# A hybrid decoder trunk on one core: attention with token-major values and 64-row score products, column sums in one wide product, pooling in quadrants

## The chip, the core and the metric

The kernel runs on one core of a Trainium2 chip. The metric is the device time of one execution in microseconds. The kernel before took 896.11 us as the median of three runs (891.52, 896.11, 896.16).

The engines are named as the profile names them: PE is TensorE (PEld its weight loads), DVE VectorE, ACT ScalarE, POOL GpSimd, SP the queue that issues most transfers.

## The reference, cut to what matters

All data is f32. One layer over 1024 tokens of width 1024: a normalised and modulated input `h` is projected by `w_in`; the columns of the projection feed four mixers (pooling, sliding-window attention, gated convolution, RWKV time mixing); their outputs are joined, projected by `w_out` and added to x. A mixture of 32 experts follows. The change lies in the projection, the attention, the pooling, and in the modulation vector that the second half of the layer needs.

```python
mod = cond @ w_ada[l] + b_ada[l]          # six vectors of 1024: sh1 sc1 gt1 sh2 sc2 gt2
p = h @ w_in[l]
# attention: 4 query heads, 2 key/value heads of 64, window 128, blocks of 128 tokens
qb = q.reshape(B, nb, 128, KVH, G, hd) * (hd ** -0.5)
s = jnp.einsum('bnqhgd,bnkhd->bnhgqk', qb, kb)     # k over this block and the one before
s = s - slopes[:, :, None, None] * dist            # and masked by the window
p = exp(s - m); p = p / (sum(p) + exp(sink - m))
o = jnp.einsum('bnhgqk,bnkhd->bnqhgd', p, vb)
# pooling: 4 groups of 64 channels, each with a 64x64 matrix
y = jnp.einsum('btgc,gce->btge', d, w_pool)
```

## The kernel before, in words

The program is written engine by engine; every dependence is a semaphore, and the order on each engine is the order of the code.

**Projection.** `project` (L853) makes one block of 128 projected columns for all 1024 tokens: the stationary operand is a 128x128 tile of `w_in` (`win[:, par, k, :]`), the moving one is 512 tokens of `hT` (the input, channels on the partitions), two halves by eight steps of k, 16 products in PS banks 0 and 1 or 2 and 3. ACT moves out the first half of the tokens and DVE the second (`projected`) into `pT`, which is [channel, block, token]. There are 19 blocks in the order of `ORDER`: two of queries, the keys, the values (i = 3), then pooling, convolution and RWKV.

**Attention in slots.** From block i = 5 on, each `project` has a piece of the attention beside it (L931 to L952), and this document calls that stretch a slot. In a slot PE runs, in this order: `outputs(nb)` (probabilities by values), `scores(nb + 2)`, the first half of a `project`, `flip_probs(nb + 1)` (the probabilities turned by 8 transposes), `sums(nb + 2)`, the second half of the `project`. A Fori loop of two turns holds the slots nb = 0 to 3; the slots nb = 4 and 5 are written out behind it, and the slots for nb = 6 and 7 have only `outputs`, `project` and, for the first, `flip_probs`.

- `scores` (L871) takes a query tile `qz` with the 64 rows of the other key head at zero (ACT builds it in `queries`, with the factor 1/8), so each of the 4 heads is one product over all 128 rows with 256 keys. Then it transposes two tiles of values (`vs`, copied by ACT) into PS bank 6, from which ACT (`values`) makes `vt`.
- `outputs` (L900) makes 8 products of 128 rows by 64 columns, in the order head, key block; heads 0 and 2 land in partitions 0 to 63, heads 1 and 3 in 64 to 127.
- `sums` (L914) adds over the partitions what DVE gathered in `acb` (512 columns of the modulation per slot, `half_blocks`, L1810: 16 operations on 256 columns). For the gate vectors (nb = 0, 1, 6, 7) it is one wide product of a tile of ones by `acb`; for the shift and scale vectors (nb = 2 to 5, the slots of the loop) eight products with a single moving column each, whose stationary operand is 64 strided columns of `acb`. DVE adds the bias (`gate_columns` or `mod_columns`).

**DVE's order in a slot** (L1837): `projected`, `attended` (copy of the outputs), `softmax`, `flipped`, `mod_columns`, `half_blocks`. In `softmax` it waits for ACT's exponentials. `flip_probs` on PE waits for `att_nm` of the newest scores, which `softmax` gives once it has read them.

**Pooling and convolution** run on POOL from the moment that block 11 is projected (L620 to L650). `pooled` (L955) then multiplies each half of the pooled channels by a 128x128 matrix that holds two 64x64 blocks on its diagonal, two products of 512 tokens each; `pooled(0)` stands ahead of block 16 and `pooled(1)` behind it.

Of the kernel before, what the change touches and what calls it, by code (L numbers as in the profile page):

```python
# [114 lines left out]
def build(nc, w, out):  # L115
    ctx = ExitStack()
    with ctx:
# [38 lines left out]
        qz, o = area(REG_W, A_ATT, 4, P)  # L156
        vs, o = area(REG_W, o, 2 * P)
        vt, o = area(REG_W, o, 2, 2, P)
        sc, o = area(REG_W, o, 2, 4, 2 * P)
# [189 lines left out]
        def identb(n):  # L349
# [11 lines left out]
                 "att_q att_qk att_vps att_v  att_nm att_p att_pn att_tp att_tpa att_tpd att_o att_y "  # L361
# [418 lines left out]
        def _(pe):  # L780
# [89 lines left out]

            def scores(nb):  # L871
                first = isinstance(nb, int) and nb == 0
                k0 = 1 if first else 0
                ks = slice(nb * P + (PAD - P * (1 - k0)), nb * P + PAD + P) if isinstance(nb, int) else \
                    ds(nb * P + (PAD - P), 2 * P)
# [12 lines left out]

            def flip_probs(nb, par, nxt=True):
                k0 = 1 if isinstance(nb, int) and nb == 0 else 0  # L890
# [9 lines left out]
            def outputs(nb, par):  # L900
                k0 = 1 if isinstance(nb, int) and nb == 0 else 0
# [12 lines left out]
            def sums(nb, gates, half=0):  # L914

                pe.wait_ge(s["acb_ready"], nb * 2 + 2)
                pe.wait_ge(s["att_v"], nb + 1)
# [10 lines left out]
            for i in range(2, SLOT0):  # L928
                project(i % 2, 32 * (i // 2 + 1), i - 1, shifted=i == 2)
# [3 lines left out]
            project(1, 32 * 3, 4, lambda: sums(0, True))  # L933
            scores(1)
            project(0, 32 * 4, 5, lambda: (flip_probs(0, 0), sums(1, True)))

            def beside(g, u, gates):

                outputs(g * 2 + u, u)
                scores(g * 2 + (2 + u))  # L940
                project((1 + u) % 2, g * 32 + 32 * (4 + u), g * 2 + (6 + u),
                        lambda: (flip_probs(g * 2 + (1 + u), (1 + u) % 2), sums(g * 2 + (2 + u), gates, u)))

            with pe.Fori(0, 2) as g:
                for u in range(2):
                    beside(g, u, False)
            for u in range(2):
                beside(2, u, True)
            outputs(6, 0)
            project(1, 32 * 7, 12, lambda: flip_probs(7, 1, False))  # L950
            outputs(7, 1)
# [3 lines left out]
            def pooled(c):  # L955
# [420 lines left out]
        def _(act):  # L1376
# [43 lines left out]
            def projected(i, par, blk=None):  # L1420
# [6 lines left out]
                else:  # L1427
                    fn(dst, PS[2 * par][:, :]).then_inc(s["proj_act"], 1)


            def queries(nb):
                first = isinstance(nb, int) and nb == 0
                k0 = 1 if first else 0
                tok = slice(nb * P + PAD, nb * P + PAD + P) if isinstance(nb, int) else ds(nb * P + PAD, P)
                at = slice(nb * P + PAD - P * (1 - k0), nb * P + PAD + P) if isinstance(nb, int) else ds(nb * P + (PAD - P), 2 * P)
                if not first:
                    act.wait_ge(s["att_qk"], nb)
                    act.wait_ge(s["att_vps"], nb)
                for kv in range(2):
                    r = slice(64 * kv, 64 * kv + 64)  # L1440
                    fn(qz[r, 2 * kv:2 * kv + 2, :], pT[r, B_Q:B_Q + 2, tok], scale=float(HD) ** -0.5)
                fn(vs[:, k0 * P:], pT[:, B_VAL, at]).then_inc(s["att_q"], 1)

            def values(nb, par):
                k0 = 1 if isinstance(nb, int) and nb == 0 else 0
                act.wait_ge(s["att_vps"], nb + 1)
                fn(vt[:, par, k0:, :], PS[6][:, k0 * P:256].rearrange("p (a b) -> p a b", b=P)).then_inc(s["att_v"], 1)
# [15 lines left out]
            for i in range(2, N_ATT):  # L1463
                projected(i, i % 2)
            act.wait_ge(s["proj_dve"], N_ATT)
            act.wait_ge(s["proj_act"], N_ATT)
            for n in range(2):
                queries(n)
                projected(SLOT0 - 1 + n, n)
                values(n, n)  # L1470
# [3 lines left out]
            with act.Fori(0, 3) as g:  # L1474
                for u in range(2):
                    queries(g * 2 + (2 + u))
                    projected(g * 2 + (6 + u), u, g * 2 + (B_BG + u))
                    values(g * 2 + (2 + u), u)
# [4 lines left out]
            def pooled(c):  # L1483
                act.wait_ge(s["pool_ps"], c + 1)
# [167 lines left out]
        def _(dve):  # L1652
# [96 lines left out]
            dve.wait_ge(s["ss_ready"], NT)  # L1749
            dve.wait_ge(s["hT_tr"], NT)  # L1750
# [501 lines left out]
```

## Time and profile before

| | us |
|---|---|
| median of three runs | 896.11 |
| lowest and highest run | 891.52, 896.16 |
| span of the profiled execution | 890.9 |
| PE busy | 837.5 (94%) |
| DVE busy | 453.4 (51%) |
| POOL busy | 277.5 (31%) |
| ACT busy | 252.9 (28%) |

The profile is one execution; its span runs from the first to the last instruction, and its own total isn't given apart from it: it lies 0.6 us below the lowest run and 5.2 us below the median. PE is busy over nearly the whole span, so the reading starts with what PE does, and goes by the starts of its groups: the end of a product in the profile is modelled, the start of the next group isn't. The profile records every f32 product as two matmul records, and every transpose as one.

### The profile page before, as it was taken

What the parts mean: (1) busy time and instruction counts of PE and PEld (TensorE: products, weight loads), DVE (VectorE), ACT (ScalarE), POOL (GpSimd) and SP (SyncE); (2) the same over time, 40 slices, a digit from 0 to 9 for tenths busy, and PEclk for the clock granted to TensorE, in tenths of its full rate; (3) what the DMA queues carried; (4) which work ended last, traced back from release to release, by engine and by line L of the source; (5) the groups of instructions that cost most, each with busy time, mean ns of one, the idle gap of its engine ahead of it and who ended that gap; (6) DMA issues with size and microseconds to landing.
All of it is one profiled execution on the core that took longest, in us unless ns stands there. A gap on an engine that the chain in (4) does not pass through costs nothing.

```text
span 890.9 us, 17159 instructions
## 1 busy us (share of the span) xinstructions
PE 837.5 (94%) x7046; PEld 561.2 (63%) x7046; DVE 453.4 (51%) x1146; ACT 252.9 (28%) x613; POOL 277.5 (31%) x265
## 2 busy tenths in 40 slices
PE   5999999999999999899999999999999999999950
PEld 5754445555544444788788555555788888888830
DVE  3830467777741133667674243443664555555534
ACT  5310122222210140564543122223222322323214
POOL 4810000000099800615524000000035556544232
PEclk9899999999999999999999999999999999999985
DMA  9923543334300120300000492111889999988639
GB/s 343 282 80 102 162 136 120 118 118 142 118 24 25 47 71 0 146 3 4 4 3 5 179 403 104 47 48 56 314 296 306 295 287 272 283 263 266 211 70 368
DMA packets 79638, 136.32 MB, mean 153 GB/s; under 512 B 17134, under 2 KB 51147, under 8 KB 79563
## 3 DMA queue, kind: packets, MB, share of 16 engines
q1 hardware_dynamic: 69258, 118.44, 38.3%
q0 software_dynamic: 10304, 16.82, 7.9%
q8 instruction: 55, 0.90, 0.4%
q14 instruction: 21, 0.16, 0.1%
HBM read 124.18 MB, written 29.92 MB: 173 GB/s over the span
## 4 chain that ended last, share of the span: by engine, by line
PE 90%; DMA 3%; DVE 3%; issue 2%; ACT 1%; SPq 0%; DVEq 0%; POOLq 0%; POOL 0%; ACTq 0%
PE bank L782 84%; PE bank L1330 3%; DMA REG_Y<-in_x 2%; DVE REG_P L2227 1%; DMA REG_P<-y_d 1%; PE bank L896 1%; PE bank L1261 1%; DMA REG_Y<-xn_d,tbl 1%; DMA y_d<-REG_Y,idx 1%; PE bank L1029 0%; DVE REG_P L1969 0%; DVE REG_P L1951 0%; ACT REG_W L1378 0%; ACT REG_Y L1378 0%; PE bank L886 0%
## 5 line engine op out<-in xcount | busy, mean ns | idle before, releaser
L782 PE MATMUL bank<-REG_W 128*128 128x512 f32 (+1 forms) x736 | 273.4, 542 | 0.0
L782 PEld LDWEIGHTS bank<-REG_W 128*128 128x128 f32 (+1 forms) x736 | 118.0, 181 | 138.1 <-issue 137.6
L782 PE MATMUL bank<-REG_W,REG_Y 128*128 128x512 f32 x256 | 118.3, 599 | 1.4 <-DVE REG_Y L2182 1.1
L1378 ACT ACTIVATE REG_P<-bank 128x256 f32<-128x256 f32 (+2 forms) x126 | 53.4, 462 | 154.8 <-PE bank L782 132.1
L1378 ACT ACTIVATE REG_Y<-bank,mod,s 128x128 f32<-128x128 f32 x136 | 51.1, 456 | 86.8 <-PE bank L1330 86.8
L782 PE MATMUL bank<-REG_P 64*64 64x64 f32 (+1 forms) x2816 | 69.3, 223 | 6.5 <-issue 4.5
L782 PEld LDWEIGHTS bank<-REG_W,REG_Y 128*128 128x128 f32 x256 | 45.6, 191 | 44.3 <-issue 44.2
L782 PEld LDWEIGHTS bank<-REG_Y,REG_W 128*128 128x128 f32 (+1 forms) x640 | 65.7, 181 | 7.1 <-issue 7.1
L782 PEld LDWEIGHTS bank<-REG_P 64*64 64x64 f32 x2816 | 60.9, 134 | 14.4 <-issue 6.7
L782 PE MATMUL bank<-REG_Y,REG_W 128*128 128x128 f32 (+1 forms) x640 | 69.0, 276 | 0.2 <-DVE REG_Y L2051 0.2
L626 POOL TENSOR_TENSOR REG_P<-REG_P 128x1040 f32<-128x1040 f32 x2 | 4.8, 2390 | 187.1 <-DVE REG_P L1765 187.0
L782 PE MATMUL bank<-REG_Y,REG_P 128*128 128x128 f32 x496 | 58.2, 275 | 0.0
L782 PEld LDWEIGHTS bank<-REG_Y,REG_P 128*128 128x128 f32 x496 | 56.7, 192 | 0.7 <-issue 0.7
L1674 DVE SCALAR_TENSOR_TENSOR REG_Y<-REG_P,cc,REG_Y 128x256 f32<-128x256 f32 x112 | 54.3, 485 | 4.0
L719 POOL DMA_INDIRECT y_d<-REG_Y,tbl x22 | 34.9, 1588 | 59.9 <-DVE REG_Y L2190 59.9
L782 PE MATMUL bank<-REG_P,REG_Y 128*128 128x512 f32 x112 | 51.4, 592 | 0.0
L668 POOL TENSOR_TENSOR REG_P<-REG_P,lmask 128x512 f32<-128x512 f32 x20 | 25.8, 1300 | 78.7 <-DVE REG_P L1960 78.4
L2051 DVE TENSOR_SCALAR REG_Y<-bank,s,mod 128x128 f32<-128x128 f32 x136 | 46.2, 404 | 2.7 <-PE bank L1330 2.7
L571 POOL TENSOR_SCALAR ss<-ss 128x1 f32<-128x1 f32 x16 | 3.8, 238 | 137.2 <-ACT REG_P L1378 127.8
L2179 DVE SCALAR_TENSOR_TENSOR REG_Y<-REG_Y,bank 128x128 f32<-128x128 f32 x33 | 9.5, 288 | 70.5 <-issue 45.5
L1378 ACT ACTIVATE REG_Y<-bank 128x128 f32<-128x128 f32 (+2 forms) x43 | 14.9, 347 | 101.7 <-PE bank L782 61.7
L2190 DVE SCALAR_TENSOR_TENSOR REG_Y<-bank,tbl,gtb 128x512 f32<-128x512 f32 x46 | 32.4, 747 | 19.3 <-PE bank L782 16.8
(296 smaller groups left out, 1168.1 us busy)
## 6 DMA issues: line engine op xcount, KB each, us to landing
REG_P<-in_w_ada SPq DMA_DIRECT2D x18, 1024.0 KB, 6.3
REG_W<-in_w_in SPq DMA_DIRECT2D x17, 512.0 KB
REG_P<-in_moe_w_gate SPq DMA_DIRECT2D x17, 512.0 KB
REG_W<-in_moe_w_gate SPq DMA_DIRECT2D x16, 512.0 KB
REG_W<-in_moe_w_up SPq DMA_DIRECT2D x16, 512.0 KB
REG_W<-in_moe_w_down SPq DMA_DIRECT2D x16, 512.0 KB
REG_P<-in_moe_w_up SPq DMA_DIRECT2D x14, 512.0 KB
REG_P<-in_w_ada SPq DMA_DIRECT2D x3, 2048.0 KB, 12.4
```

What stands on the lines that cost most here:

```text
L668: gp.tensor_tensor(bl[:, l % 2], ab[:, :, 0, :], lmask[:, l:l + 1, :].to_broadcast([P, 8, CH]), ALU.mult)\
L719: gp.indirect_dma_start(out=y_d[:, :], out_offset=bass.IndirectOffsetOnAxis(ap=at, axis=0), in_=yo[b], in_offset=None, bounds_check=last_r ...
L782: return pe.matmul(o_, l, r, start=start, stop=stop, skip_group_check=True)
L896: last = pe.transpose(PS[4 + h // 2][:, ((h % 2) * 2 + kb) * P:((h % 2) * 2 + kb + 1) * P], sc[:, par, h, kb * P:(kb + 1) * P], ident[:, :])
L1261: last = pe.transpose(PS[4 + k // 4][:, (k % 4) * P:(k % 4 + 1) * P], strided[:, k, :], ident[:, :])
L1330: last = pe.transpose(PS[k // 4][:, (k % 4) * P:(k % 4 + 1) * P], xg[b][:, k * P:(k + 1) * P], ident[:, :])
L1378: return act.activation(o_, i_, f, **kw)
L1674: last = stt(dst, src[:, k], cc[:, k:k + 1], dst, ALU.mult, ALU.add)
L2051: last = ts(dst[:, k, :], PS[bank][:, (k - 4) * P:(k - 3) * P], s2[:, k:k + 1], mod[:, M_SH2 + k:M_SH2 + k + 1], ALU.mult, ALU.add)
L2179: ch.step(stt(a1[:, par, :], th[:, par, :], 1.0, PS[2 + par][:, 0:P], ALU.add, ALU.mult))
L2190: last = stt(yo[b][:, h * 512:(h + 1) * 512], PS[4 + 2 * par + h][:, :], gate(TURN[e] if isinstance(e, int) else e), gtb[:, 1, h * 512:(h ...
L2227: stt(x1[:, j], x1[:, j], rs[:, 2, j:j + 1], fg, ALU.mult, ALU.mult).then_inc(s["f_o"], 1)
```

## The change

Five edits. (1) The values (block 3) are projected with the operands swapped: the stationary tile is 128 tokens of `hT`, the moving one 128 columns of `w_in`, so they come out with tokens on the partitions, 64 products of 128 columns instead of 16 of 512; the two transposes per block, `vs`, `vt` and ACT's copies go. (2) `scores` multiplies only the 64 rows of the head's key head, for key heads 0 and 1 in turn, into banks 4 and 5; `qz` and ACT's `queries` go, the factor 1/8 is put into the copy of the query blocks. (3) `outputs` alternates between the two column halves from product to product, reads the values from `pT`, and leaves out the empty key block for nb = 0. (4) `sums` is the wide product for all eight; `mod_columns` on DVE picks the columns out of the wide result by a product with a mask of one diagonal and a reduction. (5) `pooled` makes four 64x64 products of 512 tokens instead of two full ones. PE's loop is written out, three memsets of DVE go.

```diff
+            def values(loads, done):
+                pe.wait_ge(s_win[1], loads)
+                pe.wait_ge(s["proj_act"], done)
+                pe.wait_ge(s["proj_dve"], done)
+                for j in range(NT):
+                    for k in range(KD):
+                        last = mm(PS[2 + j // 4][:, (j % 4) * P:(j % 4 + 1) * P], hT[:, k, j * P:(j + 1) * P], win[:, 1, k, :],
+                                  k == 0, k == KD - 1)
+                last.then_inc(s["proj_ps"], 1)
             def scores(nb):
...
-                pe.wait_ge(s["att_q"], nb + 1)
-                if not isinstance(nb, int) or nb >= 2:
+                if nb == 0:
+                    pe.wait_ge(s["proj_act"], N_ATT - 1)
+                    pe.wait_ge(s["proj_dve"], N_ATT - 1)
+                if nb == 1:
+                    pe.wait_ge(s["att_nm"], 1)
+                if nb >= 2:
                     pe.wait_ge(s["att_tpa"], nb - 1)
                     pe.wait_ge(s["att_tpd"], nb - 1)
-                for h in range(4):
-                    last = mm(PS[4 + h // 2][:, (h % 2) * 256 + k0 * P:(h % 2) * 256 + 256], qz[:, h, :], pT[:, B_KEY, ks])
-                last.then_inc(s["att_qk"], 1)
-                if not first:
-                    pe.wait_ge(s["mod2_ready"], nb)
-                for kb in range(k0, 2):
-                    last = pe.transpose(PS[6][:, kb * P:(kb + 1) * P], vs[:, kb * P:(kb + 1) * P], ident[:, :])
-                last.then_inc(s["att_vps"], 1)
+                for a in range(2):
+                    for kv in range(2):
+                        r = slice(64 * kv, 64 * kv + 64)
+                        last = mm(PS[4 + kv][:, a * 256 + k0 * P:a * 256 + 256], pT[r, B_Q + a, tok], pT[r, B_KEY, ks])
+                        if a == 1:
+                            last.then_inc(s["att_qk"], 1)
...
-                if isinstance(nb, int) and nb == NT - 1:
+                if nb >= 1:
                     pe.wait_ge(s["att_y"], nb)
-                for h in range(4):
-                    r = 64 * (h % 2)
+                for kv in range(2):
                     for kb in range(k0, 2):
-                        last = mm(PS[7][r:r + 64, (h // 2) * P:(h // 2 + 1) * P], vt[:, par, kb, (h // 2) * HD:(h // 2 + 1) * HD],
-                                  ptT[:, h, kb, :], kb == k0, kb == 1)
-                last.then_inc(s["att_o"], 1)
+                        at = PAD + (nb - 1 + kb) * P + kv * HD
+                        for a in range(2):
+                            last = mm(PS[7][64 * a:64 * a + 64, kv * P:(kv + 1) * P], pT[:, B_VAL, at:at + HD],
+                                      ptT[:, 2 * kv + a, kb, :], kb == k0, kb == 1)
...
+            def sums(nb):
                 pe.wait_ge(s["acb_ready"], nb * 2 + 2)
-                pe.wait_ge(s["att_v"], nb + 1)
-                if gates:
-                    last = mm(PS[6][:, :], ones[:, :], acb.rearrange("p a b -> p (a b)"))
-                else:
-                    strided = acb.rearrange("p a (q k) -> p k (a q)", k=KD)
-                    for k in range(KD):
-                        last = mm(PS[6][64 * half:64 * half + 64, k:k + 1], strided[:, k, :], ones[:, 0:1])
-                last.then_inc(s["mod2_ps"], 1)
+                if nb >= 1:
+                    pe.wait_ge(s["mod2_ready"], nb)
+                mm(PS[6][:, :], ones[:, :], acb.rearrange("p a b -> p (a b)")).then_inc(s["mod2_ps"], 1)
...
-                for h in range(2):
-                    last = mm(PS[6 + h][:, :], pw[:, c, :], pmd[:, c, h * 512:(h + 1) * 512])
-                last.then_inc(s["pool_ps"], 1)
+                for h, g in ((0, 0), (1, 1), (1, 0), (0, 1)):
+                    r = slice(64 * g, 64 * g + 64)
+                    last = mm(PS[6 + h][r, :], pw[r, c, r], pmd[r, c, h * 512:(h + 1) * 512])
+                    if h != g:
+                        last.then_inc(s["pool_ps"], 1)
...
-            dve.memset(ptT[:, :, 0, :], 0.0)
-            dve.memset(vt[:, 0, 0, :], 0.0)
-            dve.memset(qz, 0.0)
...
-                tt(mod[r, ds(g * KD + M_SH2, KD)], PS[6][r, 0:KD], pq[r, ds(g, 1), :].rearrange("p o k -> p (o k)"), ALU.add)\
+                ch.step(tt(pick[r], PS[6][r, :].rearrange("p (q k) -> p q k", k=KD),
+                           identq[r, :].unsqueeze(2).to_broadcast([64, HD, KD]), ALU.mult))
+                ch.step(dve.tensor_reduce(picked_k[r, :], pick[r].rearrange("p q k -> p k q"), AX.X, ALU.add))
+                tt(mod[r, ds(g * KD + M_SH2, KD)], picked_k[r, :], pq[r, ds(g, 1), :].rearrange("p o k -> p (o k)"), ALU.add)\
                     .then_inc(s["mod2_ready"], 1)
```

## Rows read from the trace of the kernel before

**Rows 1.** Page, the span in 40 slices: granted TensorE clock in tenths.
```profile
PEclk9899999999999999999999999999999999999985
```
**Rows 2.** Chain that ended last, 60 to 330 us, by line.
```profile
by line: PE bank L782 97.1%; PE bank L896 2.4%; PE bank L886 0.6%
```
**Rows 3.** Timeline, PE, one loop slot: start us, us, what, xrecords.
```profile
145.10 7.03 PE L782 MATMUL bank<-REG_W 128*128 128x512 f32 x16
151.97 1.04 PE L896 MATMUL bank<-ident,REG_W 128*128 128x128 f32 x8
152.94 2.08 PE L782 MATMUL bank<-ones,REG_Y 128*64 128x1 f32 x16
154.95 7.13 PE L782 MATMUL bank<-REG_W 128*128 128x512 f32 x16
162.01 1.15 PE L782 MATMUL bank<-REG_Y,REG_W 128*64 128x128 f32 x16
163.09 1.99 PE L782 MATMUL bank<-REG_P,REG_W 128*128 x8
164.92 0.38 PE L886 MATMUL bank<-ident,REG_W 128*128 128x128 f32 x2
165.14 0.59 PE L782 MATMUL bank<-REG_W 128*128 128x512 f32 x1
```
**Rows 4.** Timeline, PE, a slot behind the loop, with the wide sum.
```profile
232.98 1.02 PE L782 MATMUL bank<-REG_Y,ones 128*128 128x512 f32 x2
233.84 7.03 PE L782 MATMUL bank<-REG_W 128*128 128x512 f32 x16
240.80 1.14 PE L782 MATMUL bank<-REG_Y,REG_W 128*64 128x128 f32 x16
```
**Rows 5.** Timeline, PE, the scores of block 0.
```profile
109.31 1.05 PE L782 MATMUL bank<-REG_P,REG_W 128*128 128x128 f32 x8
110.21 0.27 PE L886 MATMUL bank<-ident,REG_W 128*128 128x128 f32 x1
110.31 7.03 PE L782 MATMUL bank<-REG_W 128*128 128x512 f32 x16
```
**Rows 6.** Timeline, PE, expert stage: products of 128 columns, each with new weights.
```profile
709.11 3.74 PE L782 MATMUL bank<-REG_Y,REG_P 128*128 128x128 f32 x32
712.68 1.88 PE L782 MATMUL bank<-REG_S,REG_Y 128*128 128x512 f32 x4
```
**Rows 7.** Timeline, PE, RWKV stage: products on 64x64 quadrants.
```profile
358.06 1.10 PE L782 MATMUL bank<-REG_W,REG_P 64*64 64x128 f32 x32 [0.27 <-DVE REG_P L1951]
359.09 1.16 PE L782 MATMUL bank<-cen,REG_P 128*128 128x128 f32 x8
```
**Rows 8.** Timeline, DVE, the same loop slot as rows 3.
```profile
145.09 1.42 DVE L1786 SCALAR_TENSOR_TENSOR REG_W<-adist,bank 128x256 f32<-128x256 f32 x4 [0.42 <-PE bank L782]
...
148.07 0.16 DVE L1792 TENSOR_SCALAR nm<-mx 128x4 f32<-128x4 f32 x1
...
150.88 1.14 DVE L1797 TENSOR_SCALAR REG_W<-REG_W,rd 128x256 f32<-128x256 f32 x4
...
155.37 0.35 DVE L1672 TENSOR_SCALAR REG_Y<-REG_P,cc 128x256 f32<-128x256 f32 x1
...
163.19 0.68 DVE L1765 COPY REG_P<-bank 128x512 f32 x1
163.79 0.41 DVE L1779 COPY REG_Y<-bank 128x256 f32 x1
```
**Rows 9.** Timeline, DVE, slot of block 0: a reduction and a read of bank 6.
```profile
111.32 0.69 DVE L1789 TENSOR_REDUCE mx<-REG_W 128x4 f32<-128x512 f32 x1
...
118.24 0.69 DVE L1821 TENSOR_TENSOR gtb<-gtb,bank 128x512 f32<-128x512 f32 x1 [2.66 <-PE bank L782]
```
**Rows 10.** Timeline, PE: the second pooling product.
```profile
319.46 1.88 PE L782 MATMUL bank<-REG_Y,pw 128*128 128x512 f32 x4
```
**Rows 11.** Timeline, POOL: its last pooling operation.
```profile
307.49 2.35 POOL L650 TENSOR_TENSOR REG_Y<-REG_Y,REG_P 128x1024 f32<-128x1024 f32 x1
```

More of the change, by code:

```diff
@@ L360, in build @@
                  "proj_k proj_ps proj_act proj_dve pad_ready acc_ready acb_ready "
-                 "att_q att_qk att_vps att_v  att_nm att_p att_pn att_tp att_tpa att_tpd att_o att_y "
+                 "att_qk att_nm att_p att_pn att_tp att_tpa att_tpd att_o att_y "
                  "pool_d pool_ps pool_y conv_y  "
@@ L878, in scores @@
+            def scores(nb):
+                k0 = 1 if nb == 0 else 0
+                tok, ks = slice(nb * P + PAD, nb * P + PAD + P), slice(nb * P + PAD - P * (1 - k0), nb * P + PAD + P)
+                if nb == 0:
[4 more added lines that the diff above has]
+                if nb >= 2:
                     pe.wait_ge(s["att_tpa"], nb - 1)
                     pe.wait_ge(s["att_tpd"], nb - 1)
-                for h in range(4):
-                    last = mm(PS[4 + h // 2][:, (h % 2) * 256 + k0 * P:(h % 2) * 256 + 256], qz[:, h, :], pT[:, B_KEY, ks])
@@ L889, in flip_probs @@
             def flip_probs(nb, par, nxt=True):
-                k0 = 1 if isinstance(nb, int) and nb == 0 else 0
+                k0 = 1 if nb == 0 else 0
                 pe.wait_ge(s["att_pn"], nb + 1)
@@ L898, in flip_probs, with outputs @@
                 last.then_inc(s["att_tp"], 1)
-            def outputs(nb, par):
-                k0 = 1 if isinstance(nb, int) and nb == 0 else 0
-                pe.wait_ge(s["att_v"], nb + 1)
+            def outputs(nb):
+                k0 = 1 if nb == 0 else 0
+                if nb == 0:
+                    pe.wait_ge(s["proj_act"], N_ATT)
+                    pe.wait_ge(s["proj_dve"], N_ATT)
                 pe.wait_ge(s["att_tpa"], nb + 1)
                 pe.wait_ge(s["att_tpd"], nb + 1)
-                if isinstance(nb, int) and nb == NT - 1:
+                if nb >= 1:
@@ L906, in outputs @@
                     pe.wait_ge(s["att_y"], nb)
[L907 to L908 removed]
+                for kv in range(2):
                     for kb in range(k0, 2):
[L910 to L924 removed]
+                        at = PAD + (nb - 1 + kb) * P + kv * HD
+                        for a in range(2):
+                            last = mm(PS[7][64 * a:64 * a + 64, kv * P:(kv + 1) * P], pT[:, B_VAL, at:at + HD],
+                                      ptT[:, 2 * kv + a, kb, :], kb == k0, kb == 1)
+                            if kv == 1 and kb == 1:
+                                last.then_inc(s["att_o"], 1)
@@ L926, in _ @@
+            def sums(nb):
+                pe.wait_ge(s["acb_ready"], nb * 2 + 2)
+                if nb >= 1:
+                    pe.wait_ge(s["mod2_ready"], nb)
+                mm(PS[6][:, :], ones[:, :], acb.rearrange("p a b -> p (a b)")).then_inc(s["mod2_ps"], 1)
             first_block()
             second_block()
-            for i in range(2, SLOT0):
-                project(i % 2, 32 * (i // 2 + 1), i - 1, shifted=i == 2)
+            project(0, 32 * 2, 1, shifted=True)
+            values(32 * 2, 2)
@@ L931, in _ @@
+            project(0, 32 * 3, 3)
             pe.wait_ge(s["sel_ready"], 1)
             scores(0)
-            project(1, 32 * 3, 4, lambda: sums(0, True))
+            project(1, 32 * 3, 4, lambda: sums(0))
             scores(1)
[L935 to L949, printed above, removed]
+            project(0, 32 * 4, 5, lambda: (flip_probs(0, 0), sums(1)))
+            for nb in range(NT - 2):
+                outputs(nb)
+                scores(nb + 2)
+                project((nb + 1) % 2, 32 * (nb // 2) + 32 * (4 + nb % 2), nb + 6,
+                        lambda: (flip_probs(nb + 1, (nb + 1) % 2), sums(nb + 2)))
@@ L950, in _ @@
+            outputs(6)
             project(1, 32 * 7, 12, lambda: flip_probs(7, 1, False))
-            outputs(7, 1)
+            outputs(7)
             project(0, 32 * 8, 13)
@@ L1427, in projected @@
                 else:
[L1428 to L1447, printed above, removed]
+                    fn(dst, PS[2 * par][:, :], scale=scale).then_inc(s["proj_act"], 1)
             def exps(nb, par):
@@ L1462, in _ @@
             first_projected(1)
[L1463 to L1466, printed above, removed]
+            projected(2, 0, scale=float(HD) ** -0.5)
+            projected(3, 1)
             for n in range(2):
-                queries(n)
                 projected(SLOT0 - 1 + n, n)
-                values(n, n)
                 exps(n, n)
@@ L1763, in projected @@
                     pT[:, ds(blk, 1), PAD + 512:PAD + 1024].rearrange("p o t -> p (o t)")
+                if blk is None and i == N_ATT - 2:
+                    ts(dst, PS[2 * par + 1][:, :], float(HD) ** -0.5, None, ALU.mult).then_inc(s["proj_dve"], 1)
+                    return
                 if blk is not None or i not in MIXED:
```

25 lines of the change are left out of this document (8 added, 17 removed).

## The prediction, written before the changed kernel was timed

> **What bounds the kernel now.** I read the page's slices first: PE is busy in tenths of nine over almost the whole span at a granted clock of nine tenths or more in nearly every slice, the upper of its two levels, 2.4 GHz [rows 1]. Then the chain of work that ended last, for the stretch the change touches: from 60 to 330 us it consists of PE alone, row after row [rows 2], and no PE wait stands in the view of waits there. So any time taken from PE's own stream in this stretch shortens the stretch one for one, until another engine comes late. Last the timeline of PE, where the starts of the groups give prices. A loop slot lasts from 145.10 to 165.14, 20.04 us [rows 3].
>
> **Unit prices.** Half a projection is 8 products of 512 columns, 16 records: 151.97 - 145.10 = 6.87 us, 0.429 a record, 0.859 a product [rows 3]. The time goes with the moving columns: 256 columns are 0.429 a product, 128 are 0.215. A series of 128-column products with new weights for each takes (712.68 - 709.11)/32 = 0.1116 us a record [rows 6], so nearly all of the weight load is hidden. A change of the array's shape also has a price: the same half projection lasts 6.87 between full products, 6.96 if the 64-column outputs follow [rows 4], and 7.06 if 64-column products stand on both sides [rows 3]. That is 0.10 for each change of shape.
> The Trainium skill (TensorEngine Tiling (Array Packing), Key Properties) says that a change of tiling mode drains the engine. The trace agrees, and 0.10 us is the size of it here.
>
> **1. Values token-major.** 64 products of 128 columns, 128 records by 0.1116 = 14.28 us [rows 6], in place of 16 by 0.859 = 13.74 [rows 3]: +0.54. All on the path. It can't be under 13.74, the columns being the same; if no load were hidden, the eight single-column products would be the nearest price, 2.01/16 = 0.126 a record [rows 3], 16.1, or +2.4. The expert rows are the same form, so I take +0.54.
> The transposes of values go: 0.10 for block 0 [rows 5], and 0.22 (164.92 to 165.14) [rows 3] for seven more: -1.64. ACT's copies go too, at nothing: PE never waits for them now.
>
> **2. Scores of 64 rows.** Now four products of 256 columns, 1.73 without the change of shape, 1.83 behind the outputs (163.09 to 164.92) [rows 3]. With rows 0 to 63 and 64 to 127 at work together there are two rounds of 0.429, 0.86, plus 0.10 on each side: 1.06. Six blocks behind outputs save 0.77 each, 4.62; block 1 saves 1.73 - 1.06 = 0.67; block 0 goes from 0.90 [rows 5] to 0.43 + 0.20, 0.27. Together -5.56. Do the tiles overlap? Sixteen products on four 64x64 quadrants take 359.09 - 358.06 = 1.03 us [rows 7]; one after the other they'd take 16 by 0.215 = 3.4. No row has two 64-row tiles over all columns, so the bounds are -5.56 and, without overlap, +1.0 (seven to ten changes of shape). I take the near end.
>
> **3. Outputs.** The order now is half 0, 0, 1, 1, 0, 0, 1, 1. Where the half changes, two products overlap, which leaves five rounds of 0.215 = 1.07, and the row has 1.08 (162.01 to 163.09) [rows 3]. Alternating from product to product leaves four rounds, 0.86: -0.22 for seven blocks, -1.54. Block 0 has half the products, two rounds, 0.43: -0.65. Together -2.19. The low bound is -0.65, if the two halves' weight loads, which share the read path, take up the overlap.
> A rule speaks against this edit: the Trainium skill (TensorE: Matmul & The Clock Gate, Part 3, What overlaps and what doesn't) says that a weight load overlaps a running product only where the row group differs. Here both halves use all rows. The 1.08 us, five rounds, is less than the eight rounds, 1.72, that even products with free loads would take one by one, so the trace doesn't bear it out for these tiles.
>
> **4. Sums.** Four slots lose the sixteen single-column records, 154.95 - 152.94 = 2.01 [rows 3], and get the wide product, 233.84 - 232.98 = 0.86 [rows 4]; the changes of shape on both sides go as well, 0.20. 1.35 by four: -5.40.
> On DVE `mod_columns` gets a product of 64x512 out of PSUM and a reduction of 512 elements, nearest rows 0.69 each [rows 9], with their waits some 1.45 us more than today. The reduction reads with a stride that no row has. Is DVE still covered? Its round in a loop slot would be: softmax from its first operation to its last, 152.02 - 145.09 = 6.93; `flipped` 0.60; `mod_columns` 1.61; `half_blocks` 163.19 - 155.37 = 7.82; the two copies 1.02 [rows 8]: 17.98 us. PE's new slot is 20.04 - 0.22 - 0.77 - 0.22 - 1.35 = 17.48. So DVE falls back by 0.5 us a slot. It starts softmax 1.4 us behind the start of the projection when the loop begins, by the same steps, and is 3.4 behind after four slots. What PE needs of it at its next stop, `flip_probs`, is that the scores are read: 3.14 us after the start of softmax (148.07 + 0.16 - 145.09) [rows 8], that is 6.5 us into the projection, and PE comes to it at 6.87. It holds with 0.3 us to spare. I cost it at nothing; every 0.1 us more in `mod_columns` beyond that costs 0.4. The other waits that move (sums for `acb`, outputs for `att_y` and the flipped tiles) have several us. Weights and `w_ada` are loaded a slot or more ahead.
>
> **5. Pooling.** Four products of 512 columns on two quadrants make two rounds of 0.859: 1.72, as long as the two full ones today (4 records of 0.429) [rows 3, 10]. Half of the work of each is gone, but only half of the array runs. Two changes of shape by 0.10, twice: +0.40. Bounds: -1.7 (if all four overlapped) and +3.8 (none). POOL isn't the bound: its last pooling operation ends at 309.84 [rows 11], and PE comes to it at 319.46 [rows 10]. PE will come 13 us sooner, POOL some 10 (it starts on a copy that DVE now makes later in its slot), which leaves 6.
>
> **Sum.** -5.56 - 2.19 - 5.40 - 1.64 + 0.54 + 0.40 = -13.85 us. Everything behind it, RWKV, output projection and experts, is started by PE's progress and moves as a whole. On the profiled execution: 890.9 - 13.85 = 877.0 us. The median of the runs lies 5.2 above that span: 896.1 - 13.8 = 882.3. I forecast 882.3.
>
> **The rivals.**
> - No overlap of 64-row tiles. For it: no row has this very shape. Against: the quadrants [rows 7]. Scores then give +1.0 instead of -5.56, pooling +3.8 instead of +0.4: -3.9, 892.2.
> - The half-width weight loads aren't hidden where the halves alternate from product to product. Then outputs take what sixteen half-width loads take in the single-column row, 2.01 [rows 3]: +0.93 by seven in place of -1.54, 8.0 worse, 890.3. The three places where the halves alternate today speak against it. The rule of the skill named under 3 would have it so.
> - DVE bounds PE in the loop, with the reduction one or two us dearer than its row: (4 by 1.5) - 0.3 = 5.7 us of stall, 888.0.
> - The other side, slower than before: the same mechanism at a price that eats all. PE stalls at `flip_probs` for what `mod_columns` is dearer, four times, less 0.3. It decides from (13.85 + 0.3)/4 = 3.5 us more than reckoned, a reduction of over 4 us where the row has 0.69 [rows 9]; at 5 us more it gives 19.7 of stall, 902.0. Against: eight elements apart is no reason in any row for six times the time.
> - It doesn't do what it says: PE's gain is taken back behind 330 us by something that isn't moved. Against: the chain there is PE as well. 896.
>
> **How the numbers follow.** Forecast as worked out, within some 3 us: 0.76. DVE stall of up to 6 us: 0.09. No overlap of 64-row tiles: 0.05. Unhidden half-width loads: 0.02. Gain lost later: 0.05. Slower: 0.03. A measurement of this kernel can tell 0.5%, 4.5 us, from no change, so faster means under 891.6: the forecast, the stall and the loads, 0.87. Within 0.5% are no overlap and the lost gain, 0.10; slower 0.03. The runs before differ by 4.6 us between themselves; if the median after falls on a low run it is 891.5 - 13.8 = 877.7, so the range goes down to 876. Upward it takes in the stall and the unhidden loads: 890.5.
>
> **What would show it.** Loop slots of 17.5 us on PE; scores groups of about 0.96 from start to start to their last round, outputs 0.86; the wide sum 0.86 in every slot; the values' 128 records in 14.3; pooling still 1.7 to 1.9. A PE wait on DVE L1792 or its like in the slots nb = 4 and 5 would be the stall; `mod_columns` of more than 1.7 us its cause. Wrong would be: scores groups of 1.8, POOL's end behind PE's arrival, or idle PE time behind 330 us that wasn't there.

## The result and the profile after

The changed kernel took 882.79 us as the median of four runs (878.94 to 884.75), the kernel before, with one more run, 894.86 (891.52 to 896.16). The ratio is 0.9871 with a 95% interval of 0.9827 to 0.9914, which lies clear of 1: faster, by 12.1 us between the medians where 13.85 was forecast. In a later comparison of six runs with eleven of before it was 0.9847 (0.9797 to 0.9897).

The profiled execution spans 882.1 us, 8.8 less than the one of before, and took 883.92 in all. So what lies around the span is 1.8 us.

| | before | after |
|---|---|---|
| span of the profiled execution, us | 890.9 | 882.1 |
| PE busy, us | 837.5 | 828.9 |
| DVE busy, us | 453.4 | 459.1 |
| ACT busy, us | 252.9 | 240.3 |

First the timeline of PE over one of the four slots that were the loop, the answer to [rows 3]: start us, duration, operation, records.

```profile
159.01 1.13 PE L781 MATMUL bank<-REG_P 64*128 64x256 f32 x8
160.08 7.13 PE L781 MATMUL bank<-REG_W 128*128 128x512 f32 x16
167.05 1.04 PE L907 MATMUL bank<-ident,REG_W 128*128 128x128 f32 x8
167.92 1.02 PE L781 MATMUL bank<-REG_Y,ones 128*128 128x512 f32 x2
168.78 7.03 PE L781 MATMUL bank<-REG_W 128*128 128x512 f32 x16
175.74 1.09 PE L781 MATMUL bank<-REG_Y,REG_P 128*64 128x128 f32 x16
176.77 1.13 PE L781 MATMUL bank<-REG_P 64*128 64x256 f32 x8
```

From scores to scores it is 176.77 - 159.01 = 17.76 us, where before had 20.04 and I expected 17.48. By the starts: the scores take 1.07, but the half projection behind them 6.97 instead of 6.87; the wide sum takes 0.86; the outputs take 1.03, where the old order took 1.08 and I expected 0.86.

The same view where block 0 has its outputs, half as many products as the other blocks:

```profile
140.67 0.66 PE L781 MATMUL bank<-REG_Y,REG_P 128*64 128x128 f32 x8
141.26 1.14 PE L781 MATMUL bank<-REG_P 64*128 64x256 f32 x8
```

The slot of block 4 has a piece of waiting in it. The same view, PE and then DVE:

```profile
213.34 7.13 PE L781 MATMUL bank<-REG_W 128*128 128x512 f32 x16
221.05 1.06 PE L907 MATMUL bank<-ident,REG_W 128*128 128x128 f32 x8 [0.58 <-DVE nm L1771]
```
```profile
206.72 0.69 DVE L1805 TENSOR_TENSOR REG_W<-bank,identq 64x512 f32<-64x512 f32 x1
207.45 1.07 DVE L1807 TENSOR_REDUCE REG_W<-REG_W 64x8 f32<-64x512 f32 x1
208.71 0.17 DVE L1808 TENSOR_TENSOR mod<-REG_W,pq 64x8 f32 x1 [0.18 <-DVE REG_W L1807]
...
217.78 1.40 DVE L1765 SCALAR_TENSOR_TENSOR REG_W<-adist,bank 128x256 f32<-128x256 f32 x4
...
220.74 0.16 DVE L1771 TENSOR_SCALAR nm<-mx 128x4 f32<-128x4 f32 x1
```

DVE begins softmax at 217.78, 4.4 us after the projection started at 213.34; `nm` is ready at 220.90 and the flip, which could have begun at 213.34 + 6.97 = 220.31, begins at 221.05. With the flip itself, 221.05 to 221.95 where it takes 0.87 elsewhere, the wait costs the path 0.77 us, a little more than the 0.58 in the brackets. The page's chain of before is 90% PE; here it is 79% PE and 10% DVE, since followed back from this flip it runs through DVE. The reduction is what I had too low: 1.07 us for 0.69.

The pooling, with the first product of the RWKV stage behind it:

```profile
292.05 1.93 PE L781 MATMUL bank<-REG_Y,pw 64*64 64x512 f32 x8
293.91 14.00 PE L781 MATMUL bank<-REG_W 128*128 128x512 f32 x32
307.84 1.93 PE L781 MATMUL bank<-REG_Y,pw 64*64 64x512 f32 x8
309.71 3.70 PE L781 MATMUL bank<-REG_W 128*128 128x512 f32 x8
313.34 0.48 PE L781 MATMUL bank<-lt,lor 32*128 32x256 f32 x1
```

1.86 us for each group, two rounds as reckoned, and nothing gained. The RWKV stage begins at 313.34, in the profile of before at 324.71: 11.4 us of the saving are there at that point, 8.8 at the end. The view of stretches shows what the clock did behind that point (columns: length and busy time of PE, PEld, DVE, ACT and POOL with their counts, granted clock, DMA share, GB/s):

```profile
315.00:320.00 5.00, 5.00 (x16) 2.60 (x15) 3.16 (x6) 2.69 (x7) 1.68 (x1) 0.66 0.00 0
395.00:400.00 5.00, 4.36 (x53) 4.06 (x53) 1.65 (x4) 0.85 (x3) 2.96 (x3) 0.85 0.02 3
400.00:405.00 5.00, 5.00 (x122) 4.98 (x124) 1.57 (x4) 1.46 (x5) 4.10 (x3) 0.50 0.01 3
405.00:410.00 5.00, 5.00 (x117) 4.19 (x114) 3.11 (x9) 3.50 (x8) 0.00 (x0) 0.96 0.02 3
```

The granted clock fell to 1.2 GHz twice in the RWKV stage. The first fall costs 5 by (1 - 0.66) = 1.7 us of PE's work, the second 0.75 + 2.5 + 0.2 = 3.45. In the profile of before the clock is 1.00 in all four stretches.

Each of the two executions also has a fall ahead of the part that was changed, first before, then after:

```profile
30.00:35.00 5.00, 5.00 (x21) 3.97 (x22) 2.48 (x7) 3.34 (x4) 4.21 (x13) 0.56 1.04 370
35.00:40.00 5.00, 5.00 (x10) 2.03 (x9) 4.82 (x7) 0.81 (x1) 4.56 (x8) 0.75 1.08 344
```
```profile
30.00:35.00 5.00, 5.00 (x28) 3.62 (x28) 3.42 (x8) 4.34 (x5) 4.34 (x11) 0.83 1.03 373
35.00:40.00 5.00, 5.00 (x11) 2.15 (x10) 4.79 (x8) 0.31 (x1) 4.49 (x9) 0.83 1.05 348
```

That is 3.45 us lost before and 1.7 after, and PE starts the projection of the keys at 68.03 before and at 67.01 after. A second profile of the changed kernel, with 3.45 us lost there, has 68.12. So 1.0 of the 11.4 us isn't the change. The change itself, from the projection of the keys to the RWKV stage, is (324.71 - 68.03) - (313.34 - 67.01) = 256.68 - 246.33 = 10.35 us.

### The profile page after: what moved, and what is told of

Read it like the earlier page. It is cut to its first block, busy times and chain, and to the rows that moved or that the text cites. A ratio compares the mean times of both kernels' runs of the same rounds, so it can differ in the third digit from the quotient of the medians.

```text
span 882.1 us, 17139 instructions
## 1 busy us (share of the span) xinstructions
PE 828.9 (94%) x7071; PEld 555.5 (63%) x7071; DVE 459.1 (52%) x1151; ACT 240.3 (27%) x581; POOL 277.6 (31%) x265
## 4 chain that ended last, share of the span: by engine, by line
PE 79%; DVE 10%; DMA 4%; issue 3%; ACT 1%; POOL 1%; SPq 0%; DVEq 0%; POOLq 0%; ACTq 0%
PE bank L781 74%; PE bank L1336 3%; DVE REG_Y L1655 3%; DMA REG_Y<-in_x 2%; DMA REG_Y<-xn_d,tbl 1%; DVE REG_P L2209 1%; DMA REG_P<-y_d 1%; ACT REG_W L1384 1%; PE bank L1267 1%; DVE REG_W L1765 1%; DVE mx L1768 1%; DMA y_d<-REG_Y,idx 1%; POOL y_d L718 1%; PE bank L1035 0%; DVE REG_W L1807 0%
## 5 line engine op out<-in xcount | busy, mean ns | idle before, releaser
L781 PE MATMUL bank<-REG_W 128*128 128x512 f32 (+2 forms) x832 | 275.8, 501 | 0.0
L781 PEld LDWEIGHTS bank<-REG_W 128*128 128x128 f32 (+1 forms) x832 | 126.6, 183 | 136.3 <-issue 135.2
L781 PE MATMUL bank<-REG_P 64*64 64x64 f32 (+3 forms) x2880 | 79.9, 231 | 5.9 <-issue 3.9
L781 PEld LDWEIGHTS bank<-REG_P 64*64 64x64 f32 (+1 forms) x2880 | 68.6, 139 | 16.1 <-issue 9.0
L781 PEld LDWEIGHTS bank<-REG_Y,REG_P 128*128 128x128 f32 (+1 forms) x616 | 63.2, 181 | 6.5 <-issue 6.5
L781 PE MATMUL bank<-REG_Y,REG_P 128*128 128x128 f32 (+1 forms) x616 | 66.5, 276 | 0.0
L781 PE MATMUL bank<-REG_Y,REG_W 128*128 128x128 f32 x512 | 59.9, 275 | 0.0
L781 PEld LDWEIGHTS bank<-REG_Y,REG_W 128*128 128x128 f32 x512 | 58.4, 192 | 0.8 <-issue 0.8
```

Source lines behind the costliest of these rows:

```text
L781: return pe.matmul(o_, l, r, start=start, stop=stop, skip_group_check=True)
```

## The experiments

All are edits of the changed kernel but two, which time the kernel before and the changed kernel once more. All but the last two kernels of the last section ran once. The single times, 877.65 to 896.40 us, differ by the clock's falls as much as by the edits, so what an edit is worth is read from its trace. "The stretch" runs from the start of the scores of block 0 to that of the scores of block 7, 230.80 - 108.95 = 121.85 us in the changed kernel.

### The order of the outputs

```diff
                 for kv in range(2):
-                    for kb in range(k0, 2):
-                        at = PAD + (nb - 1 + kb) * P + kv * HD
-                        for a in range(2):
+                    for a in range(2):
+                        for kb in range(k0, 2):
+                            at = PAD + (nb - 1 + kb) * P + kv * HD
```

> The outputs go back to the order head by head (column half 0, 0, 1, 1, ...) in the changed kernel. In the changed kernel the group of block 1 and later takes 1.02 us from start to start, block 0 (half the products) 0.59, so 0.43 for each two rounds and a fixed part of 0.16. If the order is what saves, as I forecast (five rounds against four), the group becomes 0.16 + 5 by 0.215 = 1.23 us. If the engine keeps both halves busy in either order, it stays at 1.02 to 1.07, and my 0.22 us a block was never there to be had.

A second kernel puts `for a` outermost, so that one column half is finished before the other starts.

> The outputs make all four products of column half 0 first, then the four of half 1. If products start strictly in order, only one pair can overlap: seven rounds, 0.16 + 7 by 0.215 = 1.66 us a group. If the engine takes the second half's products ahead of waiting ones, the group stays near 1.02. With a look-ahead of one product it lies between, near 1.4.

Timeline of PE, outputs and the scores behind them, in the first kernel and in the second:

```profile
157.75 1.15 PE L781 MATMUL bank<-REG_Y,REG_P 128*64 128x128 f32 x16
158.83 1.13 PE L781 MATMUL bank<-REG_P 64*128 64x256 f32 x8
```
```profile
157.95 1.58 PE L781 MATMUL bank<-REG_Y,REG_P 128*64 128x128 f32 x16
159.46 1.14 PE L781 MATMUL bank<-REG_P 64*128 64x256 f32 x8
```

The old order takes 1.08 us, the new one 1.02 or 1.03: 0.05 a block, not 0.22. With one half after the other it takes 1.51: dearer, but less than seven rounds. So my rounds, in which a product that waits for its half holds up the next one, are not what the engine does. The times are as if it got past one or two waiting products, and short runs on one half cost nearly nothing; by what means isn't shown. What I had read as a fifth round in [rows 3] is a fixed part: block 0 with half the products takes 0.59 (140.67 to 141.26), so two rounds are 0.43 and the rest, 0.16, doesn't depend on the number.

### Do the 64-row products overlap?

```diff
-                for a in range(2):
-                    for kv in range(2):
+                for kv in range(2):
+                    for a in range(2):
                         r = slice(64 * kv, 64 * kv + 64)
```

> The scores make both products of key head 0 (rows 0 to 63), then both of key head 1. Now the group takes 1.06 us: two rounds of 0.43 and 0.20. If the gain of the 64-row products is the overlap of the two row halves, neighbours in the same rows can't overlap: three rounds, 1.29 + 0.20 = 1.49 us. If 64-row products are simply faster than 128-row ones, the group stays at 1.06.

```profile
160.45 1.14 PE L781 MATMUL bank<-REG_P 64*128 64x256 f32 x8
161.53 7.13 PE L781 MATMUL bank<-REG_W 128*128 128x512 f32 x16
```

It stayed at 1.08 us (160.45 to 161.53), which by the expectation would speak for products that are fast by themselves. But the outputs had shown that short runs on one half cost nothing, so the order can't tell the two apart. All four products on the same rows can. This kernel leaves out the rows of key head 1, for queries and keys alike:

```diff
-                        last = mm(PS[4 + kv][:, a * 256 + k0 * P:a * 256 + 256], pT[r, B_Q + a, tok], pT[r, B_KEY, ks])
+                        last = mm(PS[4 + kv][:, a * 256 + k0 * P:a * 256 + 256], pT[0:64, B_Q + a, tok], pT[0:64, B_KEY, ks])
```

> All four score products read rows 0 to 63, so the scores of key head 1 are those of key head 0 (this part of the computation is left wrong; its size and all else stay). The order of the products didn't matter (1.06 to 1.08 us with the heads in turn or one after the other). If the two row halves work at the same time, and the engine takes the other half's product past a waiting one, then with one half alone nothing overlaps: 4 by 0.43 + 0.20 = 1.92 us a group, and the stretch from the scores of block 0 to those of block 7 is 7 by 0.86 longer, 127.4 us for 121.85. If products of 64 rows are fast by themselves, it stays at 1.06.

```profile
159.05 1.99 PE L781 MATMUL bank<-REG_P 64*128 64x256 f32 x8
160.97 1.55 PE L781 MATMUL bank<-REG_W 128*128 128x512 f32 x3
```

1.92 us (160.97 - 159.05), as expected of products that run one by one. The stretch is 233.49 - 106.83 = 126.66 us: 4.8 more. (The 127.4 I had written counts block 7, whose scores lie behind the end of the stretch, and block 0 in full, and leaves out that the wait on DVE goes: 6 by 0.86 + 0.43 - 0.77 = 4.8 is the right sum.) So a 64-row product is no faster than a 128-row one; the gain is the overlap of the two row halves. The first verdict, from the order, falls.

### The sums

The single-column products for the shift and scale vectors come back, without DVE's picking.

```diff
+                if 2 <= nb < 6:
+                    half = nb % 2
+                    strided = acb.rearrange("p a (q k) -> p k (a q)", k=KD)
+                    for k in range(KD):
+                        last = mm(PS[6][64 * half:64 * half + 64, k:k + 1], strided[:, k, :], ones[:, 0:1])
+                    last.then_inc(s["mod2_ps"], 1)
+                    return
...
-                ch.step(tt(pick[r], PS[6][r, :].rearrange("p (q k) -> p q k", k=KD),
-                           identq[r, :].unsqueeze(2).to_broadcast([64, HD, KD]), ALU.mult))
-                ch.step(dve.tensor_reduce(picked_k[r, :], pick[r].rearrange("p q k -> p k q"), AX.X, ALU.add))
```

> The four shift and scale sums go back to eight single-column products, and DVE's picking goes; all else stays changed. PE's slot becomes 17.76 + 1.15 + two changes of shape (0.2) = 19.1 us; DVE's round loses 2.0 us; the wait of 0.58 us goes. Stretch from the scores of block 0 to the projection behind the scores of block 7: 122.91 + 4 by 1.35 - 0.58 = 127.7 us. If the wide sum had been worth less, because DVE's picking costs PE more than the one wait, the stretch would come out under 126.

```profile
143.47 7.13 PE L781 MATMUL bank<-REG_W 128*128 128x512 f32 x16
150.44 1.04 PE L907 MATMUL bank<-ident,REG_W 128*128 128x128 f32 x8
151.41 2.08 PE L781 MATMUL bank<-ones,REG_Y 128*64 128x1 f32 x16
153.42 8.83 PE L781 MATMUL bank<-REG_W 128*128 128x512 f32 x16
162.18 1.09 PE L781 MATMUL bank<-REG_Y,REG_P 128*64 128x128 f32 x16
163.20 1.14 PE L781 MATMUL bank<-REG_P 64*128 64x256 f32 x8
...
182.30 0.92 PE L781 MATMUL bank<-REG_P 64*128 64x256 f32 x6
```

The slot from 163.20 to 182.30 lasts 19.10 us, as expected: 1.34 more than 17.76, four times 5.4. The other three last 20.8, because the granted clock fell in each (0.92 over the slot, 1.00 in the clean one); in the first, the half projection behind the sums takes 162.18 - 153.42 = 8.76 where 7.06 is its price. The stretch is 241.65 - 110.09 = 131.56 us, 9.7 more: 5.4 of the sums, less the 0.8 that the wait cost, and 3 by 1.7 = 5.1 of clock. (The expected 127.7 is for a stretch up to the projection behind the scores, 1.06 longer, and has no falls in it; 131.56 + 1.06 - 5.1 is 127.5.)

That raised a question about the kernel before: do its sums bring the clock down as well?

> The kernel before once more, for the clock. With the single-column sums put back into the changed kernel, the granted clock fell to 1.2 GHz for a while in three of the attention's four loop slots, 1.7 us each; in the profile of before it didn't fall there. If these sums are what lets it fall now and then, some loop slots of this run are longer than 20.04 us, or the clock falls at other places than in the changed kernel; a clean run has four slots of 20.04 and the stretch from the scores of block 0 to the projection behind the scores of block 7 at 134.6 us. If the falls have nothing to do with the sums, they come in the RWKV stage alone, as in the runs of the changed kernel.

They didn't in this execution: 241.99 us is the start of the scores of block 7 and 109.43 that of block 0, 132.56 us against 132.57 in the profile of before, no slot with a fall. Nor is there one in its RWKV stage; its one fall ahead of the end of the experts is that at 30 to 40 us, 3.45 us as in the first profile. (The 134.6 in the expectation is up to the projection behind the scores.) The idea isn't borne out. The eleven runs of before beside it have mean granted clocks between 0.970 and 0.982 and times between 901.8 and 891.6 us, so in some of them the clock falls more often than in the two profiles, but where can't be seen.

### DVE as the next bound

The picking is made twice.

```diff
                 ch.step(dve.tensor_reduce(picked_k[r, :], pick[r].rearrange("p q k -> p k q"), AX.X, ALU.add))
+                ch.step(tt(pick[r], PS[6][r, :].rearrange("p (q k) -> p q k", k=KD),
+                           identq[r, :].unsqueeze(2).to_broadcast([64, HD, KD]), ALU.mult))
+                ch.step(dve.tensor_reduce(picked_k[r, :], pick[r].rearrange("p q k -> p k q"), AX.X, ALU.add))
```

> The two picking operations of DVE (product with the diagonal, reduction) are made twice in each of the four loop slots: some 0.7 + 1.25 = 2.0 us more a slot. My theory: PE waits for DVE at the flip of probabilities for what DVE falls back beyond its slack, and the slack is used up (0.58 us of wait now): 0.58 + 4 by 2.0 = 8.5 us of PE wait, in the last two or three of these slots. The rival, that DVE has slack of its own elsewhere in the slot, gives a wait of under 3 us.

The view of waits, PE alone, 60 to 310 us (us in total, times, longest):

```profile
PE bank L907 <- DVE nm L1771: 7.3, 3, 2.6
```

7.3 us in three slots, 1.2 less than reckoned, and more than twice what a slack elsewhere would leave. The stretch is 236.21 - 107.03 = 129.18, 7.3 longer than in the changed kernel and 8.1 longer than without any wait (121.08, the next experiment). So what is added to DVE's round comes back on PE nearly in full.

Then the wait was taken away. `flip_probs` only needs the scores to have been read; `att_nm` comes 1.7 us later.

```diff
-                    pe.wait_ge(s["att_nm"], nb + 2)
+                    pe.wait_ge(s["att_rd"], nb + 2)
...
                 ch.wait()
+                dve.sem_inc(s["att_rd"], 1)
                 ch.step(dve.tensor_reduce(mx[:, :], sc[:, par, :, k0 * P:], AX.X, ALU.max))
```

> DVE signals that the scores have been read right behind the reads, ahead of the maximum, 1.7 us earlier than att_nm, and PE's flip waits for that. If the 0.58 us of PE wait is DVE's lag at att_nm and nothing else, it goes to 0, and the stretch from the scores of block 0 to the projection behind the scores of block 7 goes from 122.91 to 122.3 us. If DVE's lag shows at the next wait (sums, outputs), it stays at 122.9.

```profile
213.03 7.13 PE L781 MATMUL bank<-REG_W 128*128 128x512 f32 x16
220.00 1.04 PE L907 MATMUL bank<-ident,REG_W 128*128 128x128 f32 x8
```

The flip follows the half projection after 6.97 us, no PE wait is left between 60 and 310, and the stretch is 229.72 - 108.64 = 121.08, 0.77 shorter. DVE is no less late than before (softmax at 217.83, 4.80 behind the projection), and no other wait of PE notices. (The expectation's figures of 122.91 and 122.3 are for a stretch up to the projection behind the scores of block 7, 1.06 longer; the difference is what counts.)

The reduction's own price was tried by writing the product so that it reads neighbours.

```diff
-        pick, o = area(REG_W, o, HD, KD)
+        pick, o = area(REG_W, o, KD, HD)
...
-                ch.step(tt(pick[r], PS[6][r, :].rearrange("p (q k) -> p q k", k=KD),
+                ch.step(tt(pick[r].rearrange("p k q -> p q k"), PS[6][r, :].rearrange("p (q k) -> p q k", k=KD),
...
-                ch.step(dve.tensor_reduce(picked_k[r, :], pick[r].rearrange("p q k -> p k q"), AX.X, ALU.add))
+                ch.step(dve.tensor_reduce(picked_k[r, :], pick[r], AX.X, ALU.add))
```

> The picked product is written so that the reduction reads neighbouring elements; the product writes with the stride. The reduction takes 1.07 us and its result comes 0.18 later, where I had 0.69 from a row of 512 contiguous elements over 4 results. If the stride is the cause: 0.65 to 0.75 us, DVE's round 0.4 us shorter, and the PE wait of 0.58 gone. If the cause is something else (eight results, the 64 partitions), it stays at 1.07 and the wait too.

```profile
151.49 1.03 DVE L1805 TENSOR_TENSOR REG_W<-bank,identq 64x512 f32<-64x512 f32 x1 [0.17 <-PE bank L781]
152.56 0.68 DVE L1807 TENSOR_REDUCE REG_W<-REG_W 64x8 f32<-64x512 f32 x1
```

The stride is the cause: 0.68 us without it. But it costs nearly the same where it went, 1.03 us for the product instead of 0.69, so DVE's round is hardly shorter, and the other half of the expectation failed: 0.41 us of the wait remained. The Trainium skill (SBUF — State Buffer, Door 1: The DMA port swizzle) says that SBUF has lines of 16 bytes, and that each access that crosses to another line pays. Here elements lie 32 bytes apart, and the trace agrees, with 0.35 to 0.39 us for 512 of them; no run tried another step.

### The pooling, and a version with both repairs

```diff
-                for h, g in ((0, 0), (1, 1), (1, 0), (0, 1)):
-                    r = slice(64 * g, 64 * g + 64)
-                    last = mm(PS[6 + h][r, :], pw[r, c, r], pmd[r, c, h * 512:(h + 1) * 512])
-                    if h != g:
-                        last.then_inc(s["pool_ps"], 1)
+                for h in range(2):
+                    last = mm(PS[6 + h][:, :], pw[:, c, :], pmd[:, c, h * 512:(h + 1) * 512])
+                last.then_inc(s["pool_ps"], 1)
```

> The pooling products go back to two full ones of 512 tokens; all else stays changed. I read 1.86 us for the quadrant group and 0.2 us of changes of shape around it, against 1.72: the full form should be 0.34 us faster each time, 0.68 in both, from the first pooling product to the RWKV stage's first product (21.29 us now) 20.7. If the quadrants overlapped more than two deep it would be slower by up to 0.8 each.

```profile
291.92 1.88 PE L781 MATMUL bank<-REG_Y,pw 128*128 128x512 f32 x4
293.63 13.90 PE L781 MATMUL bank<-REG_W 128*128 128x512 f32 x32
...
312.61 0.48 PE L781 MATMUL bank<-lt,lor 32*128 32x256 f32 x1
```

312.61 - 291.92 = 20.69 us, 0.60 less than with quadrants, and 0.09 more goes ahead of the first group. The quadrants are a loss of 0.69 us.

Both repairs together, timed beside the changed kernel:

> The changed kernel once more, beside the two others of this call on the same chip: 882 to 883 us, 0.986 to 0.988 of before.

> Two edits on the changed kernel: the early signal that the scores are read (0.58 us of wait gone, measured 0.77 on the stretch) and the full pooling products (0.69 us). Both are on PE's path, so 1.4 us faster than the changed kernel, 0.16%: 881.2 us where that one has 882.6; less than the clock makes from run to run. If removing the wait only moves it to the next step, 0.7 us.

The changed kernel took 882.51 us (six runs, 875.51 to 885.98), ratio to before 0.9847 (0.9797 to 0.9897). The version with both repairs took 877.30 (six runs, 876.51 to 878.82), ratio 0.9794 (0.9753 to 0.9834). In their profiles the way from the scores of block 0 to the RWKV stage is 314.44 - 110.06 = 204.38 and 309.94 - 107.01 = 202.93 us: 1.45 less, what the two edits were worth one by one. The other 3.8 us between the medians are not explained by the edits. The mean granted clock of the six runs is 0.979 for the one and 0.984 for the other, and the profile of the repaired version has no fall of the clock at all before the end of the experts, where the changed kernel's has three: 3.45 us at 30 to 40 us and 1.7 twice in the RWKV stage. Of the 4.0 us between the two spans (881.0 and 877.0) 3.05 come ahead of the scores of block 0, where the first of these falls lies; behind the start of the RWKV stage the version with both repairs is 0.5 us slower, although the other two falls are not in it. Whether the fewer falls come from the edits or from chance can't be told from six runs each and one profile each.

## Why the prediction was right, step by step

The median came out at 882.8, forecast 882.3. The steps, each by PE's timeline:

| step | forecast, us | measured, us | from |
|---|---|---|---|
| values token-major | +0.54 | +0.55 | 108.95 - 80.83, less one projection of 13.83: 14.29 for 13.74 |
| transposes gone | -1.64 | -1.6 | 0.10 and seven of 0.21 or 0.22, no longer in the timeline |
| scores | -5.56 | -4.5 | six by 0.66 (1.83 + 6.87 is now 1.07 + 6.97), 0.47 for block 1, 0.06 for block 0 |
| outputs | -2.19 | -0.9 | seven by 0.05 or 0.06, block 0 0.49 |
| sums | -5.40 | -5.4 | 19.10 against 17.76, four times |
| pooling | +0.40 | +0.69 | full products put back |
| wait on DVE | 0 | +0.77 | taken away |
| sum | -13.85 | -10.35 | |

The sum of the measured terms is the 10.35 us by which PE's path from the projection of the keys to the RWKV stage is shorter in the profile.

- **What bounds the kernel** was right: what was taken from PE's stream came through one for one, less the one wait on DVE. POOL was never waited for in the pooling: its last pooling operation ends at 300.95 and PE comes to it at 307.84, 6.9 us to spare where I had put 6.
- **Sums and values**, whose prices stood in the rows of before in the same form, came out to 0.1 us.
- **Outputs** is the step that failed in its mechanism. I explained 1.08 us as five rounds because the arithmetic fitted; it is four rounds and a fixed part, and the order is worth a quarter of what I said. The row of block 0 in the new kernel, half the products, is what tells it. The rule of the Trainium skill (TensorE: Matmul & The Clock Gate, Part 3, What overlaps and what doesn't) that I weighed there, that a weight load overlaps a running product only where the row group differs, isn't borne out by this trace: the 128 records of the values use all rows and have new weights each, and take 14.29 us, 0.1116 a record, where the moving columns alone take 6.87/64 = 0.107. What it would cost the alternating halves never showed: 1.03 us a group is 0.05 less than the old order.
- **Scores** was right in its mechanism, shown by the products on the same rows, and 1.1 us too high: a group on part of the array costs about 0.4 us, 0.1 ahead, 0.2 inside and 0.1 behind, where I had put 0.2.
- **Pooling**: right that quadrants save no round, short by the same fixed part.
- **DVE** is the term that I put at nothing. I had it 3.4 us late at the end of the loop with 0.3 to spare. It was 1.0 late at the loop's start (softmax at 143.27, the projection at 142.32) and 4.4 four slots on, so it fell back by 0.9 us a slot and not by 0.5: the reduction took 1.07 and not 0.69, and its result comes 0.18 after it, while PE's slot was 0.28 longer than forecast, which gives some of it back. The wait stands at the place and in the slot that I named, block 4. The rival of a DVE stall came true in its mechanism, at 0.8 us where I had put 5.7; the slower one, which needed 3.5 us more a slot, was far off.
- **No overlap** and **unhidden loads** are out: 1.07 and 1.03 us a group, 14.29 for the values.
- **Nothing behind 330 us changes** was right for the work, but the time there isn't constant. From the RWKV stage's start to the end it is 566.2 us before and 568.8 after, with falls worth 5.1. Executions of the edited kernels without a fall there have 564.4 to 567.1, and one with a fall of 1.7 has 563.7, so the falls are not all of the spread.

So the path is worth 10.35 us, and the medians differ by 12.1, and 12.4 in the second comparison. The remainder of 1.7 to 2.0 us isn't explained; the clock's falls, which differ from run to run, are large enough for it, but that isn't shown. That the forecast met the median within 0.5 us is part luck: the sum was 3.5 us too high, and against that stand the unexplained 1.7 us and a median of before that came out 1.25 us lower with a fourth run (894.86 for 896.11).

## What to carry to other kernels

Where PE is the bound, price an edit by starts of groups, and look for a row with half the number of products: it splits a group's time into a part that goes with the number and a fixed part, and only the first is to be had by a better order. Products on part of the array pay if their number of rounds falls (scores: four to two) and lose if it doesn't (pooling). And when PE's slot shrinks, lay the next engine's round beside it with the wait's exact place: here a strided reduction 0.4 us dearer than its row, in each of four slots, was more than the 0.6 us that PE waited, and the repair was to signal what the waiting instruction needs, not what comes three operations later.

## What the runs showed of the hardware that was not expected

- Products on different parts of the array overlap in nearly any short order: alternating 1.02 us, two and two 1.08, four and four 1.51 for the same eight products.
- A group on part of the array has a fixed part inside, 0.16 us for the outputs, 0.21 for the scores (1.07 for two rounds of 0.43), 0.14 for the pooling quadrants (1.86 for two rounds of 0.86), besides 0.1 us on either side.
- The granted clock also falls to 1.2 GHz while PE is busy without a gap (5.00 of 5 us, at 30 to 40 us and in the slots of the single-column sums), for 1.7 us of lost work or a multiple of it, at places that differ between executions of one kernel. With the single-column sums it fell in three of the four loop slots of one execution, and in none of these slots in two executions of the kernel before, which has the same sums. At 30 to 40 us, ahead of everything that was changed, the two profiles of the kernel before lose 3.45 us each, the two of the changed kernel 1.7 and 3.45, and the repaired version nothing. What brings it about stays open.
